# Conditioning projection of a two-block transformer kernel: as two-column products among the attention units, or as a GpSimd sum beside the feed-forward

## The chip, the cores and the metric
One NeuronCore of one Trainium2 chip runs the whole program in one launch. The metric is device microseconds of an execution, median of the runs. The engines are TensorE (PE, with weight loads shown as PEld), VectorE (DVE), ScalarE (ACT), GpSimd (POOL) and SyncE (SP), which issues most DMAs. Each runs its own instructions in program order and waits on semaphores for the others.

## What is computed
Two layers of a first block, then one layer of a second block, on 512 tokens of 1024 features, in float32. The part that the change touches is `mod`, the conditioning projection that the second block needs at its beginning. It depends on the inputs alone, so it may be formed at any time before.

```python
def first_block(x, ...):
    for l in range(2):
        # three attentions on rms_norm(x): MLA (6 heads, 96 wide), differential
        # (4 heads x 2 maps, 64 wide, values 128 wide), GQA (6 query heads, 64 wide)
        x = x + mix @ w_o[l]
        gate, up = jnp.split(_rms_norm(x, ffn_norm[l]) @ w_gate_up[l], 2, axis=-1)
        x = x + (jax.nn.silu(gate) * up) @ w_down[l]        # 2816 hidden

def second_block(x, c, ctx, c_ctx, w_ada, b_ada, ...):
    mod   = (silu(c)     @ w_ada[0] + b_ada[0])[:, None, :]  # 6 * 1024 values
    mod_c =  silu(c_ctx) @ w_ada[0] + b_ada[0]               # the first 2 * 1024 are used
    sh1, sc1, g1, sh2, sc2, g2 = jnp.split(mod, 6, axis=-1)
    ...
```

## The kernel before
Activations lie feature-major: 8 tiles of 128 features by 512 tokens. Each engine's order is written out by hand, in one function for each engine, and counters of semaphores tie them together.

A layer of the first block runs: input projection (split into high and low float32r parts), then three attentions one after the other, differential, GQA, MLA, then the output projection, then the feed-forward (FFN). An attention is a loop over units (`attend` on PE, `softmaxes` on ACT): one unit is one head or map by 128 queries, 32 units in the differential attention, 24 in GQA and in MLA. In step j PE transposes the exponentials of unit j (4 transposes of 128x128), forms the scores of unit j + 3 (one product of 512 columns in float32, of 64 rows in the differential attention and in GQA, of 96 in MLA), and multiplies values for unit j - 1 (4 products, 128 columns wide in the differential attention, 64 in GQA and MLA). DVE finds each row's maximum, ACT takes the exponential and copies the transposes out of PSUM. An attention is entered through a block of transposes that bring heads into feature-major form, which ACT copies out.

The 48 x 128 columns of `w_ada` go through the three-slot weight `ring` in 24 pieces of 256 columns (`ada_piece`, 1 MB each), 12 a layer, between the MLA weights and `w_o`. `modulation` on PE takes one: 8 products with `cvec`, the two silu'd vectors, as the stationary operand of two columns, 256 columns moving. ACT copies the 2x256 row out, `modulation_columns` transposes it in two 2-row transposes, and ACT copies 128x4 into `mod`. One piece is taken ahead of an attention's first scores, and three more at the steps of `ADA_AT`.

The FFN has 38 pieces of weights, 22 of gate and up (q < FT) and 16 halves of down. SP loads raw weights into two buffers `raws`, ACT copies the high part (`split_high`), DVE subtracts (`split_low`), PE multiplies, three float32r products for each tile (48 a gate/up piece, 33 a down half). SP issues the load of piece q when the split of piece q - 2 is done. POOL has no work in the FFN; it forms the low parts of the input weights, rotates GQA's and MLA's heads, and issues the small loads.

Of the kernel before, what the change touches and what calls it, by code (L numbers as in the profile page):

```python
# [80 lines left out]
def build(nc, A, out):  # L81
    ctx = ExitStack()
    with ctx:
# [6 lines left out]

        xT = sb("xT", [P, KT, S])
        C = sb("C", [P, 2944])
        ident = sb("ident", [P, P])
# [81 lines left out]
        ptmp = R[:, 11904:12288].rearrange("p (a c) -> p a c", a=2)  # L175
        mod_row = R[0:2, 12544:12800]
        SQ = R[:, 13056:14208].rearrange("p (a c) -> p a c", a=2)
# [95 lines left out]

        ADA_AT = {(32, 0): (3, 12, 22), (24, 32): (2, 9, 16), (24, 56): (2, 9, 16)}
        AW = 256

# [20 lines left out]
        piece_high, piece_low = sem("piece_high"), sem("piece_low")  # L297
        c_in = sem("c_in")
        gqa_inv_ready = sem("gqa_inv_ready")
        bT_ready, gT_ready, aT_ready = sem("bT_ready"), sem("gT_ready"), sem("aT_ready")  # L300
# [45 lines left out]
        def quarter_pieces(what, a, n):  # L346
# [6 lines left out]
                + quarter_pieces("gqa_kv", c1 + 3 * BH * BV + GH * GD, 2 * GK * GD))  # L353
        L_PIECES = len(W_IN) + 2 + 6 * D // AW // L + len(WO[0])

# [5 lines left out]
        def layer_pieces(l):  # L361
            w = A["w_in"][l]
            for _, a, n in W_IN:
                yield lambda i, a=a, n=n: [(slot(i, KT, n), cols(w, a, a + n))]
            yield lambda i: [(slot(i, 3, AH * AQK), cols(A["mla_w_uq"][l], 0, AH * AQK))]
            yield lambda i: [(slot(i, 2, AH * 128), cols(A["mla_w_ukv"][l], 0, AH * 128))]
            for a in range(NADA):
                yield ada_piece(l * NADA + a)
# [3 lines left out]
        def ada_piece(a):  # L372
            return lambda i: [(slot(i, KT, AW), cols(A["w_ada_2"][0], a * AW, (a + 1) * AW))]

        NADA = 6 * D // AW // L

# [97 lines left out]
        def _(pool):  # L474
# [67 lines left out]
            for l in range(L):  # L542
# [13 lines left out]
                for t in range(TT):  # L556
                    norm_rope_A(pg, nc.gpsimd, l, t, ptmp)

            pg.more(x_ready, KT * 2 * L)
            pool.dma_start(tribias, A["c_tribias"]).then_inc(tab_in, 16)  # L560
# [15 lines left out]
        def _(pe):  # L576
# [67 lines left out]

            def modulation():

                i = weights()
                bank = ab.fill(pe)
                group(ab, bank[0:2, 0:AW], [(cvec[:, k, :], slot(i, KT, AW)[:, k, :]) for k in range(KT)]).then_inc(a_full, 1)
                read_by.append((a_full, ab.n))  # L650
                return ab.n

            def modulation_columns(taken):

                pe.wait_ge(a_free, taken)
                bank = ab.fill(pe)
                for m in range(AW // P):
                    ins = nc.tensor.transpose(bank[:, 2 * m:2 * m + 2], mod_row[:, m * P:(m + 1) * P], ident[0:2, 0:2])
                ins.then_inc(a_full, 1)

            def attend(units, l):
# [16 lines left out]

                evacuated = ab.n
                rows_taken = modulation()  # L680
                pe.wait_ge(a_free, evacuated)
                if u0 >= 1:
# [23 lines left out]
            def layer(l):  # L706
# [58 lines left out]
                read_by.append((a_full, ab.n))  # L765
                if l == 0:
                    pp.more(cs_ready)
                attend([(QK[c * 64:c * 64 + 64, h, t * P:(t + 1) * P], QK[c * 64:c * 64 + 64, 4 + h, :],
# [44 lines left out]
            def ffn(l, sums):  # L813
# [16 lines left out]
                for q in range(NF):  # L830
# [9 lines left out]
                    else:  # L840
# [7 lines left out]
                        if a == 0:  # L848
                            ins.then_inc(half_read, 1)
                            f_by.append((half_read, l * KT + (q - FT) // 2 + 1))  # L850
                        else:
                            ins.then_inc(d_full, 1)
                            f_by.append((d_full, db.n))
                            if (q - FT) // 2 >= 2:
                                sums = norm_sums(X, TT, [(q - FT) // 2 - 2], sums)
                norm_sums(X, TT, [KT - 2, KT - 1], sums)

            for l in range(L):
# [271 lines left out]
        def _(sp):  # L1130
# [13 lines left out]
            def load_ffn(l):  # L1144
                up_down = FFN_W[l]
                sp.wait_ge(*read_by[(n - 1) // NSLOT * NSLOT])
                for q in range(NF):
# [25 lines left out]
        def _(act):  # L1173
# [10 lines left out]
            raw_count = [0, 0]  # L1184
            ada = 0

# [19 lines left out]
            def softmaxes(N):  # L1206
                nonlocal unit, ada
                u0 = unit
# [5 lines left out]

                def take_rows():
                    bank = ab.take(act)
                    copy_out(mod_row, bank[0:2, 0:AW], a_free)

                take_rows()
                columns_due = True  # L1220
                expo(u0)
                expo(u0 + 1)
                for j in range(N):
# [3 lines left out]
                    copy_out(PTb[:, (u0 + j) % 2, :], bank[:, :], a_free)  # L1227
                    if columns_due:
                        bank = ab.take(act)
                        copy_out(mod[:, 2 * ada:2 * ada + 2, :], bank[:, 0:4].rearrange("p (a b) -> p a b", b=2), a_free)  # L1230
                        ada += 1
                        columns_due = False
                    if j in ADA_AT[N, unit % 80]:
                        take_rows()
                        columns_due = True
                unit += N
# [105 lines left out]
            def ffn_silu(l):  # L1342
# [18 lines left out]
                for q in range(NF):  # L1361
# [8 lines left out]
                    if q >= FT and (q - FT) % 2:  # L1370
                        square((q - FT) // 2)

            for l in range(L):
# [152 lines left out]
        def _(dve):  # L1526
# [4 lines left out]
            vp.do(v.memset(eps[:, :], EPS), setup)  # L1531
            vp.do(v.memset(ss[:, :, :], 1.0))

            def set_gains():
# [204 lines left out]
            sh1, sc1, g1, sh2, sc2, g2 = range(0, 48, KT)  # L1739
            dve.wait_ge(vec_in, 16 * N_VEC)  # L1740
            vp.do(v.tensor_tensor(mod[:, :, :], mod[:, :, :], bc(bada[:, :], 2, 2), ALU.add))
            for j, (g, sc, c) in enumerate(((0, sc1, 0), (0, sc1, 1), (1, sc2, 0))):
# [252 lines left out]
```

## Time and profile before

| | us |
|---|---|
| median of 3 runs | 3435.35 (3433.83 to 3438.79) |
| profiled execution, span from first to last instruction | 3426.4 |
| median less the span | 8.95 |
| PE busy in the span | 3252.0 (95%) |
| DVE, ACT, POOL busy | 1119.9, 995.3, 279.3 |
| share of the chain that ended last on PE | 89% |

The time of an execution is measured around the program, so it is a little above the span of a profiled one. The trace gives each instruction's start and length, and for idle time of an engine what released it. The chain of waits is followed back from the last instruction, so a stretch of it on PE is time that nothing hides. The granted clock of PE has two levels, 1.00 for 2.4 GHz and 0.50 for 1.2 GHz. The mean over the span is 0.959. A float32 product shows in the trace as two instructions of each kind, so 8 products are x16.

### The profile page before, as it was taken

What the parts mean: (1) busy time and instruction counts of PE and PEld (TensorE: products, weight loads), DVE (VectorE), ACT (ScalarE), POOL (GpSimd) and SP (SyncE); (2) the same over time, 40 slices, a digit from 0 to 9 for tenths busy, and PEclk for the clock granted to TensorE, in tenths of its full rate; (3) what the DMA queues carried; (4) which work ended last, traced back from release to release, by engine and by line L of the source; (5) the groups of instructions that cost most, each with busy time, mean ns of one, the idle gap of its engine ahead of it and who ended that gap; (6) DMA issues with size and microseconds to landing.
All of it is one profiled execution on the core that took longest, in us unless ns stands there. A gap on an engine that the chain in (4) does not pass through costs nothing.

```text
span 3426.4 us, 35084 instructions
## 1 busy us (share of the span) xinstructions
PE 3252.0 (95%) x14020; PEld 2219.0 (65%) x14020; DVE 1119.9 (33%) x1827; ACT 995.3 (29%) x1607; POOL 279.3 (8%) x268
## 2 busy tenths in 40 slices
PE   7999998999989999989999999979998999989997
PEld 6866564888878656658887555544666433468886
DVE  2624332333226343233332233344333100043322
ACT  4355441222233545322221223333222100022222
POOL 4480000000032700000000000000000000000000
PEclk8999999999989999999999999989998999989999
DMA  4221121333222211123323201102111121123331
GB/s 105 79 80 38 38 75 37 99 98 88 85 82 76 74 38 53 47 78 96 93 84 92 80 14 36 37 1 62 37 37 50 25 74 49 49 62 98 95 90 62
DMA packets 340274, 221.98 MB, mean 65 GB/s; under 512 B 8364, under 2 KB 334892, under 8 KB 340112
## 3 DMA queue, kind: packets, MB, share of 16 engines
q1 hardware_dynamic: 337360, 214.65, 21.6%
q0 software_dynamic: 2224, 2.99, 0.8%
q8 instruction: 112, 1.84, 0.2%
q10 hardware_dynamic: 528, 2.10, 0.2%
q14 instruction: 50, 0.41, 0.0%
HBM read 217.62 MB, written 2.10 MB: 64 GB/s over the span
## 4 chain that ended last, share of the span: by engine, by line
PE 89%; DVE 5%; ACT 4%; issue 1%; DMA 1%; DVEq 0%; ACTq 0%; SPq 0%
PE ps L591 83%; PE ps L602 4%; PE ps L618 2%; DVE R L1691 1%; ACT R L1204 1%; DVE xL L1687 0%; DVE x_lows L1687 0%; DMA ident<-in_c_ident 0%; PE ps L945 0%; DMA R<-in_ctx 0%; ACT R L1200 0%; ACT L1193 0%; DVE R L1780 0%; DVE R L1762 0%; DVE wL L1713 0%
## 5 line engine op out<-in xcount | busy, mean ns | idle before, releaser
L591 PE MATMUL ps<-R 128*128 128x64 f32 (+6 forms) x2272 | 519.6, 372 | 29.5 <-ACT R L1204 8.7
L591 PEld LDWEIGHTS ps<-R 128*128 128x128 f32 (+3 forms) x2272 | 306.1, 192 | 243.8 <-issue 137.1
L591 PE MATMUL ps<-xH,wH 128*128 128x512 f32 x1056 | 417.5, 395 | 21.9 <-DVE xL L1687 21.9
L591 PE MATMUL ps<-U,ring 128*128 128x512 f32 (+5 forms) x960 | 406.8, 575 | 12.3 <-ACT R L1410 12.3
L1204 ACT ACTIVATE R<-ps 128x512 f32<-128x512 f32 (+9 forms) x504 | 248.7, 493 | 578.7 <-PE ps L591 514.6
L591 PE MATMUL ps<-xL,wH 128*128 128x512 f32 x1056 | 414.2, 392 | 0.0
L591 PE MATMUL ps<-xH,wL 128*128 128x512 f32 x1056 | 414.0, 392 | 0.0
L591 PE MATMUL ps<-R,ring 128*128 128x512 f32 x704 | 367.2, 676 | 2.9 <-DVE R L1927 1.6
L1354 ACT ACTIVATE wH<-raws 128x2048 fp32r<-128x2048 f32 (+1 forms) x114 | 192.9, 1692 | 569.0 <-PE ps L591 568.4
L591 PEld LDWEIGHTS ps<-U,ring 128*128 128x128 f32 (+2 forms) x960 | 179.6, 191 | 214.7 <-issue 189.5
L1713 DVE TENSOR_TENSOR wL<-raws,wH 128x2048 fp32r<-128x2048 f32 (+1 forms) x114 | 229.3, 2011 | 233.2 <-ACT wH L1354 226.3
L591 PEld LDWEIGHTS ps<-R,ring 128*128 128x128 f32 x704 | 133.4, 193 | 203.3 <-issue 199.1
L591 PEld LDWEIGHTS ps<-xH,wH 128*128 128x128 f32 x1056 | 199.9, 189 | 77.8 <-issue 20.2
L591 PE MATMUL ps<-ring_parts,U_parts 128*128 128x256 f32 (+1 forms) x1152 | 215.2, 290 | 15.1 <-DVE x_lows L1687 15.1
L591 PEld LDWEIGHTS ps<-xH,wL 128*128 128x128 f32 x1056 | 200.2, 190 | 41.8
L591 PEld LDWEIGHTS ps<-xL,wH 128*128 128x128 f32 x1056 | 200.4, 190 | 40.4
L591 PE MATMUL ps<-hH,wH 128*128 128x512 f32 x528 | 207.2, 392 | 0.0
L591 PE MATMUL ps<-ring,U 128*128 128x256 f32 x768 | 189.8, 392 | 17.8 <-DVEq L55 17.3
L591 PE MATMUL ps<-hH,wL 128*128 128x512 f32 x528 | 205.7, 390 | 0.0
L591 PE MATMUL ps<-hL,wH 128*128 128x512 f32 x528 | 205.5, 389 | 0.0
L591 PEld LDWEIGHTS ps<-ring_parts,U_parts 128*128 128x128 f32 x1152 | 184.2, 197 | 22.0 <-issue 12.3
L591 PEld LDWEIGHTS ps<-ring,U 128*128 128x128 f32 x768 | 142.9, 193 | 59.8 <-issue 20.3
(279 smaller groups left out, 3281.8 us busy)
## 6 DMA issues: line engine op xcount, KB each, us to landing
raws<-in_w_gate_up SPq DMA_DIRECT2D x88, 512.0 KB, 5.1
ring<-in_w_in SPq DMA_DIRECT2D x36, 1024.0 KB, 6.2
ring<-in_w_ada SPq DMA_DIRECT2D x24, 1024.0 KB, 5.1
raws<-in_w_down SPq DMA_DIRECT2D x32, 704.0 KB, 4.6
raws<-in_w_ffn_in SPq DMA_DIRECT2D x44, 512.0 KB, 5.2
ring<-in_w_in SPq DMA_DIRECT2D x34, 512.0 KB, 5.7
raws<-in_w_ffn_out SPq DMA_DIRECT2D x16, 704.0 KB, 4.7
ring<-in_w_o SPq DMA_DIRECT2D x5, 1280.0 KB, 5.9
```

The source lines that it names most:

```text
L591: return nc.tensor.matmul(o, a, b, start=first, stop=last)
L602: ins = nc.tensor.transpose(bank[0:rows_, t * P:(t + 1) * P], v, ident[:, :])
L618: ins = nc.tensor.matmul(bank[:, t:t + 1], src(k)[:, t * P:(t + 1) * P], ones[:, 0:1], start=k == 0 and t == 0, stop=k == KT - 1, skip_gro ...
L1204: ap.do(f(dst, src, ACT.Copy), sem)
L1354: ap.do(f(wH[:, g % 2, 0:n], raws[:, g % 2, 0:n], ACT.Copy), wh_ready)
L1691: vp.do(v.scalar_tensor_tensor(t, xT[:, k, :], gain(k), inv, ALU.mult, ALU.mult), scaled if shift is None else None)
L1713: vp.do(v.tensor_tensor(wL[:, g % 2, 0:n], raws[:, g % 2, 0:n], wH[:, g % 2, 0:n].bitcast(F32), ALU.subtract), wl_ready)
```

## The change
The 24 products with `cvec` and their transposes leave the attentions, and the ada pieces leave the ring. In the two FFNs of the first block, behind the products of weight pieces q = 5 to 28, there is now one ada piece each: a column tile of 128 outputs for one of the two vectors, 24 a layer (`ADA`: tiles 0 to 15 for both vectors, 16 to 47 for the first alone). SP loads it (512 KB) into one of two buffers `ada_raw`, behind the raw weights of q, after the piece two before has been read. POOL multiplies its 8 x 128 columns by the 8 values of the vector and adds halves three times (512, 256, 128 columns). PE multiplies the 128x128 result by a column of ones into bank 7, and ACT copies one column into `mod`. Layers end with PE waiting for the last of these reads, and DVE waits for all 48 ahead of its use of `mod`. POOL's scratch for DMA descriptors is halved to make room for the buffers.

```diff
-        ADA_AT = {(32, 0): (3, 12, 22), (24, 32): (2, 9, 16), (24, 56): (2, 9, 16)}
-        AW = 256
+        ADA = [(m, 0) for m in range(16)] + [(m, 1) for m in range(16)] + [(m, 0) for m in range(16, 48)]
+        ADA_FIRST, N_ADA = 5, len(ADA) // L
...
+        def ada_at(l, q):
+            a = l * N_ADA + q - ADA_FIRST
+            return a if l < L and 0 <= q - ADA_FIRST < N_ADA else None
...
+                pool.wait_ge(cs_ready, 1)
+                for a in range(l * N_ADA, (l + 1) * N_ADA):
+                    w = ada_half(a)
+                    pool.wait_ge(ada_in[a % 2], 16 * (a // 2 + 1))
+                    w_ = w.rearrange("p (k c) -> p k c", k=KT)
+                    pg.do(nc.gpsimd.tensor_tensor(w_, w_, bc(cvec[:, :, ADA[a][1]], P, 2), ALU.mult))
+                    for n in (4, 2, 1):
+                        pg.do(nc.gpsimd.tensor_tensor(w[:, 0:n * P], w[:, 0:n * P], w[:, n * P:2 * n * P], ALU.add),
+                              ada_summed if n == 1 else None)
...
-                group(ab, bank[0:2, 0:AW], [(cvec[:, k, :], slot(i, KT, AW)[:, k, :]) for k in range(KT)]).then_inc(a_full, 1)
...
+            def modulation(a):
+
+                pe.wait_ge(ada_summed, a + 1)
+                if a >= 1:
+                    pe.wait_ge(ada_read, a)
+                mm(psum[7][:, 0:1], ada_half(a)[:, 0:P], ones[:, 0:1], True, True).then_inc(ada_full, 1)
...
-                evacuated = ab.n
-                rows_taken = modulation()
-                pe.wait_ge(a_free, evacuated)
+                pe.wait_ge(a_free, ab.n)
...
-                    if rows_taken:
-                        modulation_columns(rows_taken)
-                        rows_taken = None
-                    if j in ADA_AT[N, unit % 80]:
-                        rows_taken = modulation()
...
+                    if ada_at(l, q) is not None:
+                        a = ada_at(l, q)
+                        if a >= 2:
+                            sp.wait_ge(ada_read, a - 1)
+                        sp.dma_start(ada_half(a).rearrange("p (k c) -> p k c", k=KT),
+                                     cols(A["w_ada_2"][0], ADA[a][0] * P, (ADA[a][0] + 1) * P)).then_inc(ada_in[a % 2], 16)
...
+                    if ada_at(l, q) is not None:
+                        m, c = ADA[ada_at(l, q)]
+                        ap.more(ada_full)
+                        ap.do(f(mod[:, m, c:c + 1], psum[7][:, 0:1], ACT.Copy), ada_read)
```

PE at the start of GQA in the first layer, before. `ps0` to `ps2` take transposes and ada products, `ps5` to `ps7` scores, `ps3` and `ps4` values; a row with `ident` is transposes.

```order
L602 MATMUL ps2<-ident,R 64x128 x4
L591 MATMUL ps0<-ring,cvec 2x256 x8
L591 MATMUL ps7<-R 128x512
L591 MATMUL ps5<-R 128x512
L591 MATMUL ps6<-R 128x512
L602 MATMUL ps1<-ident,R 128x128 x4
L591 MATMUL ps7<-R 128x512
L658 MATMUL ps2<-ident,R 128x2 x2
L602 MATMUL ps0<-ident,R 128x128 x4
L591 MATMUL ps5<-R 128x512
L591 MATMUL ps4<-R 128x64 x4
```

The same place in the changed kernel.

```order
L616 MATMUL ps0<-ident,R 64x128 x4
L605 MATMUL ps7<-R 128x512
L605 MATMUL ps5<-R 128x512
L605 MATMUL ps6<-R 128x512
L616 MATMUL ps1<-ident,R 128x128 x4
L605 MATMUL ps7<-R 128x512
L616 MATMUL ps2<-ident,R 128x128 x4
L605 MATMUL ps5<-R 128x512
L605 MATMUL ps4<-R 128x64 x4
```

The product with `cvec` between the transposes and the first scores, and the two column transposes behind the fourth, are gone; all else keeps its order. PE in the first layer's FFN, behind gate/up piece 5, in the changed kernel:

```order
L605 MATMUL ps4<-xH,wH 128x512
L605 MATMUL ps4<-xL1,wH 128x512
L605 MATMUL ps4<-xH,wL 128x512
L605 MATMUL ps7<-ones,ada_raw 128x1
L605 MATMUL ps0<-xH,wH 128x512
L605 MATMUL ps0<-xL0,wH 128x512
L605 MATMUL ps0<-xH,wL 128x512
```

One product of one column now stands between two pieces; before, the row with `ps0` followed the one with `ps4`. SP from the MLA weights on in the first layer, before:

```order
L1141 DMA ring<-in_mla_w_ukv 128x2x768
L1141 DMA ring<-in_w_ada_2 128x8x256 x12
L1141 DMA ring<-in_w_o 128x10x384 x2
L1141 DMA ring<-in_w_o 128x10x256
L1154 DMA raws<-in_w_gate_up 128x8x128 x44
```

And in the changed kernel, from the last `w_o` piece on:

```order
L1141 DMA ring<-in_w_o 128x10x256
L1154 DMA raws<-in_w_gate_up 128x8x128 x12
L1164 DMA ada_raw<-in_w_ada_2 128x8x128
L1154 DMA raws<-in_w_gate_up 128x8x128 x2
L1164 DMA ada_raw<-in_w_ada_2 128x8x128
L1154 DMA raws<-in_w_gate_up 128x8x128 x2
```

The ada loads moved from the ring, ahead of `w_o`, to behind the raw weights of each of 24 FFN pieces, and so ahead of the raw weights of the next one.

## Rows read from the trace of the kernel before

**Rows 1.** Chain in order of time, first layer's differential attention: start us, us, what
```profile
243.99 5.68 PE ps L591 x26
...
253.20 2.14 PE ps L591 x10
...
255.78 2.14 PE ps L591 x10
```

**Rows 2.** Timeline, MLA start: start us, us, engine, line, operation, tiles
```profile
424.00 4.35 ACT L1204 ACTIVATE R<-ps 96x512 f32<-96x512 f32 x7
...
430.79 2.84 PE L591 MATMUL ps<-R 96*128 96x512 f32 x6
```

**Rows 3.** Timeline, GQA start in the first layer; in brackets idle before, and releaser
```profile
337.42 0.31 ACT L1331 ACTIVATE ssO<-ssO,eps 128x16 f32<-128x16 f32 x1
...
339.15 1.28 ACT L1212 ACT_TABLE_LOAD   x1 [1.02 <-DVE nmax L1589]
...
341.28 1.11 PE L602 MATMUL ps<-ident,R 128*128 128x128 f32 x4 [1.22 <-ACT R L1212]
```

**Rows 4.** Windows: stretch, us, PE, PEld, DVE, ACT, POOL busy, PE's clock, DMA
```profile
231.40:242.00 10.60, 10.57 (x28) 5.74 (x28) 2.46 (x5) 4.33 (x11) 9.74 (x12) 0.50 0.01 2
341.20:354.30 13.10, 13.02 (x36) 7.41 (x36) 1.83 (x4) 5.11 (x13) 0.00 (x0) 0.50 0.04 13
354.30:358.10 3.80, 3.80 (x10) 1.10 (x10) 1.14 (x3) 0.00 (x0) 0.00 (x0) 0.50 0.00 0
358.20:359.70 1.50, 1.50 (x8) 0.42 (x5) 0.00 (x0) 0.00 (x0) 0.00 (x0) 1.00 0.00 0
1259.30:1272.40 13.10, 13.03 (x36) 7.41 (x36) 1.83 (x4) 5.10 (x13) 0.00 (x0) 0.50 0.05 15
1272.40:1276.20 3.80, 3.80 (x10) 1.10 (x10) 1.14 (x3) 0.00 (x0) 0.00 (x0) 0.50 0.00 0
```

**Rows 5.** Chain in order of time, first layer's GQA, to MLA's transposes
```profile
329.30 4.30 PE ps L602 x32
...
345.74 3.90 PE ps L591 x10
...
350.50 9.29 PE ps L591 x26
...
385.03 2.09 PE ps L591 x10
...
387.56 2.09 PE ps L591 x10
...
420.34 6.82 PE ps L602 x48
```

**Rows 6.** Timeline, PE at the second layer's differential start
```profile
1146.73 3.62 PE L591 MATMUL ps<-ring,cvec 128*2 128x256 f32 x16
...
1154.41 0.66 PE L602 MATMUL ps<-ident,R 128*128 128x128 f32 x4 [1.30 <-ACT R L1212]
```

**Rows 7.** Chain in order of time, down projection of the first layer
```profile
893.36 15.13 PE ps L591 x66
909.27 15.13 PE ps L591 x66
```

**Rows 8.** Groups by form, POOL: line, operation, tiles, count, busy us, mean ns
```profile
L440 POOL TENSOR_TENSOR R<-R 128x384 f32<-128x384 f32 x8 | 8.0, 996 | 0.6
...
L440 POOL TENSOR_TENSOR R<-R 128x128 f32<-128x128 f32 x8 | 3.6, 453 | 0.6
```

**Rows 9.** Timeline, input projection of the second layer, DVE beside POOL
```profile
963.72 4.50 POOL L537 TENSOR_TENSOR ring_parts<-ring,ring_parts 128x2048 fp32r<-128x2048 f32 x1 [699.18 <-ACT ring_parts L1251]
...
965.47 3.31 DVE L1687 TENSOR_TENSOR x_lows<-R,U_parts 128x512 fp32r<-128x512 f32 x1
...
969.59 0.69 DVE L1687 TENSOR_TENSOR x_lows<-R,U_parts 128x512 fp32r<-128x512 f32 x1
```

**Rows 10.** Page, DMA issues: tiles, queue, count, KB each, us to landing
```profile
raws<-in_w_gate_up SPq DMA_DIRECT2D x88, 512.0 KB, 5.1
```

More of the change, by code:

```diff
@@ L91, in build @@
         xT = sb("xT", [P, KT, S])
+        ada_raw = sb("ada_raw", [P, 2, KT * P])
         C = sb("C", [P, 2944])
@@ L175, in build @@
         ptmp = R[:, 11904:12288].rearrange("p (a c) -> p a c", a=2)
-        mod_row = R[0:2, 12544:12800]
         SQ = R[:, 13056:14208].rearrange("p (a c) -> p a c", a=2)
@@ L298, in build @@
         c_in = sem("c_in")
+        ada_in = [sem("ada_in0"), sem("ada_in1")]
+        ada_summed, ada_full, ada_read = sem("ada_summed"), sem("ada_full"), sem("ada_read")
         gqa_inv_ready = sem("gqa_inv_ready")
@@ L353, in build @@
                 + quarter_pieces("gqa_kv", c1 + 3 * BH * BV + GH * GD, 2 * GK * GD))
-        L_PIECES = len(W_IN) + 2 + 6 * D // AW // L + len(WO[0])
+        L_PIECES = len(W_IN) + 2 + len(WO[0])
         def piece_parts(i, n):
@@ L366, in layer_pieces, with ada_half @@
             yield lambda i: [(slot(i, 2, AH * 128), cols(A["mla_w_ukv"][l], 0, AH * 128))]
-            for a in range(NADA):
-                yield ada_piece(l * NADA + a)
             for a, e in WO[l]:
                 yield lambda i, a=a, e=e: [(slot(i, 10, e - a), cols(A["w_o"][l], a, e))]
-        def ada_piece(a):
-            return lambda i: [(slot(i, KT, AW), cols(A["w_ada_2"][0], a * AW, (a + 1) * AW))]
-        NADA = 6 * D // AW // L
+        def ada_at(l, q):
+            a = l * N_ADA + q - ADA_FIRST
+            return a if l < L and 0 <= q - ADA_FIRST < N_ADA else None
+        def ada_half(a):
+            return ada_raw[:, a % 2, :]
         def second_pieces():
@@ L643, in tokens @@
                         .then_inc(ring_.filled, 1)
-            def modulation():
-                i = weights()
-                bank = ab.fill(pe)
-                group(ab, bank[0:2, 0:AW], [(cvec[:, k, :], slot(i, KT, AW)[:, k, :]) for k in range(KT)]).then_inc(a_full, 1)
[L650 to L659, printed above, removed]
+            def modulation(a):
[3 more added lines that the diff above has]
+                mm(psum[7][:, 0:1], ada_half(a)[:, 0:P], ones[:, 0:1], True, True).then_inc(ada_full, 1)
             def attend(units, l):
@@ L765, in layer @@
                 read_by.append((a_full, ab.n))
-                if l == 0:
-                    pp.more(cs_ready)
                 attend([(QK[c * 64:c * 64 + 64, h, t * P:(t + 1) * P], QK[c * 64:c * 64 + 64, 4 + h, :],
@@ L855, in ffn @@
                                 sums = norm_sums(X, TT, [(q - FT) // 2 - 2], sums)
+                    if ada_at(l, q) is not None:
+                        modulation(ada_at(l, q))
                 norm_sums(X, TT, [KT - 2, KT - 1], sums)
+                if l < L:
+                    pe.wait_ge(ada_read, (l + 1) * N_ADA)
             for l in range(L):
@@ L1184, in _ @@
             raw_count = [0, 0]
-            ada = 0
             def square(k):
@@ L1206, in softmaxes @@
             def softmaxes(N):
-                nonlocal unit, ada
+                nonlocal unit
                 u0 = unit
@@ L1213, in expo @@
                             accum_out=rsum[:, u % 4:u % 4 + 1]), s_exp)
[L1215 to L1220, printed above, removed]
                 expo(u0)
@@ L1227, in softmaxes @@
                     copy_out(PTb[:, (u0 + j) % 2, :], bank[:, :], a_free)
[L1228 to L1235, printed above, removed]
                 unit += N
@@ L1371, in ffn_silu @@
                         square((q - FT) // 2)
+                    if ada_at(l, q) is not None:
+                        m, c = ADA[ada_at(l, q)]
+                        ap.more(ada_full)
+                        ap.do(f(mod[:, m, c:c + 1], psum[7][:, 0:1], ACT.Copy), ada_read)
             for l in range(L):
@@ L1532, in _ @@
             vp.do(v.memset(ss[:, :, :], 1.0))
+            vp.do(v.memset(mod[:, 16:48, 1:2], 0.0))
             def set_gains():
@@ L1740, in _ @@
             dve.wait_ge(vec_in, 16 * N_VEC)
+            dve.wait_ge(ada_read, len(ADA))
             vp.do(v.tensor_tensor(mod[:, :, :], mod[:, :, :], bc(bada[:, :], 2, 2), ALU.add))
@@ L1983 @@
     from concourse.bass_utils import run_bass_kernel_spmd
-    nc = bacc.Bacc("TRN2", target_bir_lowering=False, num_devices=1)
+    nc = bacc.Bacc("TRN2", target_bir_lowering=False, num_devices=1, dynamic_dma_scratch_size=8192)
     arrays, views = {}, {}
```

## The prediction
> **What bounds the kernel now.** TensorE (PE) is busy 95% of the span, and the chain of waits that ended last lies on it for 89%, so I asked of each stage that the diff touches what PE itself pays there. First the chain in order of time through the attentions. In the first layer's differential attention [rows 1] a unit without an ada product takes 255.78 - 253.20 = 2.58 us, and PE never waits in it. The unit with a product and the one after it, which carries its column transposes, take 253.20 - 243.99 = 9.21 us. One ada piece thus costs 9.21 - 2 x 2.58 = 4.05 us of PE's own time, and nothing hides it. The other two attentions repeat the pattern at 2.53 us (GQA, [rows 5]) and 2.14 us (MLA) a unit, with the same 4.05 for a piece. Then the starts of the attentions [rows 2, 3, 6], where PE waits for ScalarE (ACT), and the table of windows with PE's granted clock [rows 4].
>
> That table decides the case. At the start of the first differential attention PE stands still up to 231.40 and its clock has fallen to 0.50 (the 1.2 GHz level); it works 10.57 of 10.60 us at that level and is back at 2.4 GHz at 242. At the start of GQA the clock falls too. There PE works 13.02 of 13.10 us at 0.50, with no ada product in it, and the clock doesn't come back. It comes back at about 358.1, while the ada product runs (354.30 to 358.10 at 0.50, 358.20 to 359.70 at 1.00). The second layer does the same: 13.03 of 13.10 us of attention units at 0.50, then the product, and in it the return at about 1276.3. So in both layers what PE did when the clock rose in GQA was the ada product, and no GQA unit was ever seen to bring it back. GQA units at full clock do keep it [rows 5].
>
> **What is removed.** 24 pieces: 4 in each of six attentions, one ahead of the first scores and three among the units.
> - Differential, both layers: 3 x 4.05 = 12.15, and for the first piece only its column transposes, 0.3, since the first exponential waits for ACT and VectorE (DVE), not for the product: -12.45 each, **-24.9**.
> - MLA, both layers: 12.15 again. Its first product stands ahead of the scores, which start at 430.79 [rows 2]; without it they wait only for ACT's last copy, 424.00 + 4.35 = 428.35, so they start 2.3 earlier; with the transposes 2.7. -14.85 each, **-29.7**.
>
> **GQA, the term that turns the sign.** Its start first [rows 3]: ACT ends the root at 337.42 + 0.31 = 337.73, and then waits for a maximum of scores that stood behind the product; table load to first transposes takes 341.28 - 339.15 = 2.13. Without the product the scores are there by then, and PE begins at about 337.77 + 2.13 = 339.90, 1.38 earlier. But PE has then stood still longer: its transposes end at 329.30 + 4.30 = 333.60 [rows 5], three score products follow, and then nothing until 339.9, where before it had only the 1.22 us ahead of 341.28. The clock fell even with the product there, so I take it to fall again, in both layers. Now nothing like the product follows. A GQA unit at 0.50 takes 350.50 - 345.74 = 4.76 us [rows 5] against 387.56 - 385.03 = 2.53. All 24 at the low level: 24 x 4.76 = 114.2, less the score products that the last three units don't have (three take some 2.6 at full clock, [rows 2], 5.1 at half) = 109.1. End 339.90 + 109.1 = 449.0, where before it was 420.34: +28.7. The method holds for before: 24 x 2.53 - 2.6 = 58.1, pieces 3 x 4.05 + 0.3 = 12.5, and half of the 16.8 us at 0.50 (341.28 to 358.1) = 8.4, together 79.0; the trace has 420.34 - 341.28 = 79.1. Two layers: **+57.4**. MLA's transposes, 48 in a row, then begin at the low level; they are dense and of full height, and I take the clock to return in them; some 5 us of them at half clock that ACT's copies would otherwise allow faster: 1.8 each, **+3.6**.
>
> The Trainium skill, "TensorE: Matmul & The Clock Gate", section "Part 1: The HAM clock gate", says that the default state is throttled and that sustained matmul activity releases it. Read as "PE without gaps", it has GQA back at full clock about as soon as the differential attention. By that rule this term would be -33.8 in place of +57.4; the 13 us of gapless work at 0.50 in each layer [rows 4] speak against that reading.
>
> **Differential attention of the second layer.** Before, PE had a product up to 1146.73 + 3.62 = 1150.35 and only 1.30 us of idle ahead of its first transposes [rows 6], and the clock stayed at 1.00. Without the product it stands still from 1146.73 to 1154.41 but for three score products. The nearest row is the first layer's start, with its stop before 231.40. Bounds: 0 if the clock holds, 5.3 if it costs what 10.6 us at half clock do [rows 4]. I take **+5.0**. The first layer's start has this loss already.
>
> **What is added, in the two feed-forwards (FFN) of the first block.** PE: 48 products with a one-column moving operand. The nearest is the sum of squares, four of them between two down-projection tiles: 909.27 - 893.36 - 15.13 = 0.78 us [rows 7], 0.195 each; the upper bound is that each one alone costs all 0.78. 9.4 or 37; I take the lower since the four have the same shape and also interrupt a stream: **+9.5**.
> GpSimd (POOL) [rows 8]: its adds take 453 ns at 128 elements and 996 at 384, so 2.1 ns an element more: 0.45, 0.73 and 1.27 us for the adds of 128, 256 and 512, and 2.36 for the multiply of 1024, if its broadcast costs nothing more. 4.8 us a piece, 5.1 with its waits. Pieces come once in a gate/up tile (48 products x 0.229 = 11 us) or a down half (15.13 / 2 + 0.4 + 0.2 = 8.2), on an engine that has nothing else there.
> SP: each ada load stands ahead of the next raw weight load and waits for the read of the piece two before, which ACT does after its split of the next weights, some 2.4 us into a tile. Load 5 to 6 us [rows 10], with the raw load beside it. A piece then is ready at about 2.4 + 0.4 + 5.7 + 5.1 = 13.6 us, wanted after two down halves, 16.4; the raw weights behind it land 9 us in and are split 4 us later, wanted at 16.4 too. Slack 2.8 us, in gate/up 8. ACT's 48 copies of one column lie in its idle time.
> DVE: one row shows a subtraction with both inputs in SBUF taking 3.31 us where it takes 0.69 [rows 9]; it ended 0.56 us after the POOL operation beside it. So a POOL multiply can hold up DVE's low split, and DVE's 1.6 to 2.3 us split can hold up a POOL step: up to 2 us each, within the slack. The Trainium skill, "SBUF — State Buffer", section "SBUF: two separate sides", has the same as a lock held for a whole instruction, not a shared rate; the trace agrees with the lock. Shared at equal rates, the subtraction would have lost 0.7, not 2.6, and neither changes the sum.
> The smaller scratch for POOL's own DMAs can only delay POOL's small loads; the rotations that follow them are not wanted before GQA, some 60 us later: 0, and a few us if that cover failed.
>
> **The sum** against the profiled execution: -24.9 - 29.7 + 57.4 + 3.6 + 5.0 + 9.5 = +20.9 on its span of 3426.4. The median is 8.95 above that span, and this rest stays. 3435.35 + 20.9 = **3456 us**.
>
> **Rivals.**
> - GQA comes back to full clock without a product (the skill's reading, or since the clock doesn't fall). For it: full-clock GQA units hold the clock, and the differential units brought it back. Against: [rows 4], twice. Price a layer: 339.90 + 58.1 + 5.3 of a start at half clock = 403.3, so -17.0, and the 3.6 of the transposes gone: 20.9 - 57.4 - 34.0 - 3.6 = -74, **3361 us**. This is the other side. The point from which it decides: without GQA the sum is -40, so the sign turns where a layer's GQA costs +20, that is 37 us more than here, 16.6 units at 2.23 beyond the 2.4 units' worth of its start: with fewer than 19 of the 24 units at half clock the change gains. Chance 0.11.
> - The same in one layer only: 3456 - 47 = **3409 us**. 0.05.
> - The FFN loop is longer than two down halves (POOL and DVE hold each other up at each step, loads land late). 2 us over in each of 14 pairs: **3484 us** at most, about 3470 with half of it. 0.09.
> - MLA starts at, or falls to, the low level too and stays there, as GQA does: its units have 64-column products as well. About 2 us for each of 24 units, 48 a layer: **3552 us**. 0.04.
> The rest, 0.71, is the forecast. That the change doesn't do what it says is no case: the products are gone from the attentions' order and stand in the feed-forwards'.
>
> **Range.** The forecast's own terms give 3456 with -12 (5.0 and 3.6 at zero, the clock's return by chance a few us sooner) and +27 for the one-column products at their upper bound. 3440 to 3484 holds it and the FFN rival, 0.80; outside are both faster cases and the MLA one. A measurement tells 0.2%, some 7 us: faster 0.16, within 0.04, slower 0.80.
>
> **What would show it.** Granted clock 0.50 through all of GQA in both layers, units at 4.76, 1.00 again within MLA's transposes; differential and MLA units at 2.58 and 2.14 with no 9.21 pairs; a fall of the clock at the second layer's first start. In FFN 48 POOL groups of about 5 us and PE idle near none in front of ps<-ada_raw. I am wrong if the clock in GQA is at 1.00 after some 10 us, or if PE waits for POOL.

## The result, and the profile after

| | before | after |
|---|---|---|
| median, us (runs) | 3435.38 (4) | 3465.05 (4) |
| lowest to highest | 3433.83 to 3438.79 | 3459.97 to 3467.24 |
| profiled span | 3426.4 | 3465.4 |
| mean granted clock | 0.959 | 0.926 |

The changed kernel is slower: ratio 1.0084, 95% interval 1.0070 to 1.0099. The forecast was 3456 (3440 to 3484), slower. The profiled executions differ by 39.0 us, the medians by 29.7; more on that below.

First a correction. The text on record counts 48 ada pieces, 24 a layer, behind q = 5 to 28. The list `ADA` has 16 + 16 + 32 = **64** entries: tiles 0 to 15 for both vectors and 16 to 47 for one. So there are 32 pieces a layer, behind q = 5 to 36, 17 in gate/up and 15 in the down halves, and DVE waits for 64. The page of after has the count:

```profile
L568 POOL TENSOR_TENSOR ada_raw<-ada_raw,cvec 128x1024 f32<-128x1024 f32 x64 | 123.8, 1935 | 1047.4 <-DMA ada_raw<-in_w_ada 1047.4
```

Windows of after, PE alone (stretch, us, PE busy, PE's clock, DMA): GQA of the first layer, MLA's transposes behind it, the second layer's differential start, GQA of the second layer.

```profile
331.80:435.80 104.00, 104.00 (x325) 0.50 0.00 1
436.00:441.00 5.00, 5.00 (x25) 0.51 0.01 3
1161.30:1181.00 19.70, 19.70 (x45) 0.50 0.15 51
1264.80:1372.00 107.20, 107.19 (x330) 0.50 0.00 1
```

These answer to [rows 4]. Before, the stretch at 0.50 ended inside the ada product. Now PE works 104.00 of 104.00 us and 107.19 of 107.20 without a gap, and stays at the 1.2 GHz level to the end of GQA. The Trainium skill, "TensorE: Matmul & The Clock Gate", "Part 1: The HAM clock gate", has sustained matmul activity release the throttle. Read as "PE is busy", the trace refutes it twice; which products are at work when the clock does rise is asked below.

The chain of after at the start and the end of the first layer's GQA:

```profile
330.11 0.66 PE ps L616 x4
...
332.86 3.90 PE ps L605 x10
...
337.62 3.90 PE ps L605 x10
```

```profile
427.08 0.85 PE ps L616 x4
...
436.14 5.03 PE ps L616 x24
```

A unit takes 337.62 - 332.86 = 4.76 us, as in the slow pair of [rows 5], all the way. GQA's first transposes to MLA's take 436.14 - 330.11 = 106.0 us, against 420.34 - 341.28 = 79.1 before.

Stage by stage, the two profiled executions:

| stage | change, us | predicted |
|---|---|---|
| differential, first layer | -10.8 | -12.45 |
| GQA, first layer (with its start) | +25.5 | +28.7 |
| MLA, first layer (with its transposes) | -13.7 | -13.05 |
| all attentions and projections of the second layer | +7.5 | +8.2 |
| FFN, first layer | +10.8 | +4.7 |
| FFN, second layer | +10.6 | +4.7 |
| second block and last FFN, from the loading of `ctx` on | +8.1 | 0 |

An attention is counted from the block of transposes ahead of it to the next one's, MLA to the FFN's first product. The 1.0 us that the table lacks lies ahead of the first differential attention. Within the second layer the differential attention changed by -5.2, GQA by +26.9, MLA by -13.4, and what is ahead of them by -0.8.

### The profile page after: what moved, and what is told of

It reads as the page before. It is cut to its first block, busy times and chain, and to the rows that moved or that the text cites. A ratio compares the mean times of both kernels' runs of the same rounds, so it can differ in the third digit from the quotient of the medians.

```text
span 3465.4 us, 34885 instructions
## 1 busy us (share of the span) xinstructions
PE 3281.0 (95%) x13716; PEld 2267.4 (65%) x13716; DVE 1136.1 (33%) x1828; ACT 992.6 (29%) x1623; POOL 604.9 (17%) x524
## 4 chain that ended last, share of the span: by engine, by line
PE 83%; DVE 5%; ACT 5%; DMA 5%; issue 1%; POOL 0%; SPq 0%; ACTq 0%; DVEq 0%; POOLq 0%
PE ps L605 77%; DMA raws<-in_w_down 4%; PE ps L616 4%; PE ps L632 1%; ACT wH L1345 1%; ACT R L1209 1%; DVE R L1687 1%; DVE xL L1683 0%; DVE x_lows L1683 0%; DVE wL L1709 0%; DMA ident<-in_c_ident 0%; PE ps L945 0%; DMA R<-in_ctx 0%; DMA ada_raw<-in_w_ada 0%; ACT L1198 0%
## 5 line engine op out<-in xcount | busy, mean ns | idle before, releaser
L605 PE MATMUL ps<-R 128*128 128x64 f32 (+6 forms) x2272 | 601.4, 416 | 36.5 <-ACT R L1209 16.1
L605 PEld LDWEIGHTS ps<-R 128*128 128x128 f32 (+3 forms) x2272 | 353.6, 220 | 287.5 <-issue 161.6
L1209 ACT ACTIVATE R<-ps 128x512 f32<-128x512 f32 (+8 forms) x480 | 239.4, 499 | 520.0 <-PE ps L605 448.1
L1709 DVE TENSOR_TENSOR wL<-raws,wH 128x2048 fp32r<-128x2048 f32 (+1 forms) x114 | 239.0, 2096 | 298.7 <-ACT wH L1345 291.9
L568 POOL TENSOR_TENSOR ada_raw<-ada_raw,cvec 128x1024 f32<-128x1024 f32 x64 | 123.8, 1935 | 1047.4 <-DMA ada_raw<-in_w_ada 1047.4
L570 POOL TENSOR_TENSOR ada_raw<-ada_raw 128x512 f32<-128x512 f32 (+2 forms) x192 | 201.6, 1050 | 15.1
```

Source lines behind the costliest of these rows:

```text
L568: pg.do(nc.gpsimd.tensor_tensor(w_, w_, bc(cvec[:, :, ADA[a][1]], P, 2), ALU.mult))
L570: pg.do(nc.gpsimd.tensor_tensor(w[:, 0:n * P], w[:, 0:n * P], w[:, n * P:2 * n * P], ALU.add), ada_summed if n == 1 else None)
L605: return nc.tensor.matmul(o, a, b, start=first, stop=last)
L1209: ap.do(f(dst, src, ACT.Copy), sem)
L1709: vp.do(v.tensor_tensor(wL[:, g % 2, 0:n], raws[:, g % 2, 0:n], wH[:, g % 2, 0:n].bitcast(F32), ALU.subtract), wl_ready)
```

## Experiments

Each kernel below is the changed one with one edit, unless it says otherwise. Runs of before beside them: 3434.14 (10 runs), 3434.81 (9) and 3435.19 (9).

### A tall product in GQA, and a low one

Is it the ada product that brought the clock back, and what about it? In step 3 of each GQA:

```diff
+ bank = ab.fill(pe)
+ for n in range(8):
+     c = n % 4 * 256
+     mm(bank[0:2, 0:256], ones[0:rows, 0:2], V[0:rows, n // 4, c:c + 256], True, True)
```

with rows = 128 ("tall") and rows = 64 ("low").

> The changed kernel plus 8 products in each GQA attention, ahead of the transposes of its fourth unit: 2 stationary columns (of the ones), 256 moving columns, 128 rows high, float32, result not read. This is the shape of the ada product that was taken away. Theory 1 (GQA's units, with scores and transposes' outputs only 64 rows or columns, don't bring the clock back, the tall product did): the clock rises during the product, about 354 in the first layer, and the units behind it take 2.53 us. A layer's GQA then takes about 3 x 4.75 + 6 + 20.5 x 2.53 = 72 us in place of 106, and MLA's transposes start at full clock: 2 x 34 + 3.6 less, about 3394 us. Theory 2 (something else in the removed edit held the clock, for instance the column transposes, the extra copies on ACT, or the traffic of the ring): the clock stays at 0.50 and the time is 3465 + 2 x 6.8 = 3479.

> As the one with 8 added products in each GQA, with the same columns and the same time on PE, but 64 rows high in place of 128. Theory 1a (the clock's return goes by how many of the array's rows work): it stays at 0.50 through GQA in both layers, and the time is 3465 + 2 x 6.8 = 3479. Theory 1b (it goes by long stretches of moving columns between short pieces, whatever their height): the clock returns as with the tall product, about 3394 us.

Measured: tall **3392.22** us (0.988 of before, 0.9865 to 0.9895), low **3480.18** (1.0133, 1.0119 to 1.0147). The expectations were 3394 and 3479. The chain of tall, then of low:

```profile
336.93 9.34 PE ps L606 x26
346.27 0.59 PE ps L617 x4
346.87 2.09 PE ps L606 x10
...
349.40 2.09 PE ps L606 x10
```

```profile
338.20 10.81 PE ps L606 x26
...
350.06 3.90 PE ps L606 x10
...
354.82 3.90 PE ps L606 x10
```

The piece x26 is the product with its neighbours. Behind the tall one units take 2.53 us, behind the low one 4.76, with the same columns and PE equally without gaps. So the return needs neither the column transposes, nor ACT's copies, nor the ring's traffic, and PE's busy time doesn't decide it. Of two products alike in columns, in place and in leaving no gap, the one 128 rows high brought full clock in both layers, the one 64 rows high in neither. The low run shows where it came instead. The last three units of a GQA have no score product left, only transposes and value products, all 128 rows high and the latter still 64 columns wide. The last score product ends at 432.9, MLA's transposes begin at 441.15 (1381.85 in the second layer), and between them the clock rises:

```profile
433.00:438.00 5.00, 5.00 (x26) 0.50 0.00 0
438.10:441.10 3.00, 3.00 (x28) 1.00 0.00 0
...
1380.20:1381.80 1.60, 1.60 (x16) 1.00 0.00 0
```

Five profiled kernels leave GQA with its low scores and without a tall product (after, low, and three of the runs below: no_ada, pe_only, copy_first). In their ten GQAs the clock rose four times in these last units and six times in MLA's transposes, never in a unit with a score product of 64 rows. So values 64 columns wide don't keep the clock down by themselves. Nor does a score product of 64 rows: the differential units have one too, beside values 128 columns wide, and among them the clock came back at 246.4 in after. How the one weighs against the other within a unit isn't shown.

The removed product repaired the clock as a side effect, and one product of some 4 us was worth (3465.05 - 3392.22) / 2 = 36 us a layer, its own time paid.

### GQA's scores made tall with zeros

If height counts, the scores themselves can be made tall at no cost in instructions:

```diff
+ # DVE, unit 8 of the differential attention
+ vp.do(v.memset(QK[64:128, 13:16, :], 0.0), pad_ready)
...
+ pe.wait_ge(pad_ready, l + 1)
- attend([(QK[0:64, 8 + h, t * P:(t + 1) * P], QK[0:64, 14 + h // 3, :],
+ attend([(QK[:, 8 + h, t * P:(t + 1) * P], QK[:, 14 + h // 3, :],
```

> The changed kernel with GQA's score products made 128 rows high in place of 64, in both layers: the lower half of the array gets zeros as keys (one VectorE write of zeros a layer, beside the differential attention) and old finite data as queries, so the result is the same, the instructions on TensorE are as many and as long, and no product is added. Theory 1 (the clock's return goes by how many of the array's rows a product occupies, and zeros count): GQA starts at 0.50 and is back at full clock after some 15 to 20 us; a layer's GQA takes about 67 us in place of 106, 2 x 39 + 3.6 less: 3383 us. Theory 2 (rows fed with zeros don't count, or the long tall product was needed): no change, 3465 us.

The zeros stand in the keys; the queries have old finite values in these rows. Measured: **3354.58** us (0.9766, 0.9753 to 0.978), 110.5 less than the changed kernel, where 82 was expected; the two GQAs are 53.5 and 56.7 us shorter in the profiles. Windows, PE alone, then the chain:

```profile
334.00:338.00 4.00, 4.00 (x12) 0.60 0.00 0
338.20:384.00 45.80, 44.81 (x302) 1.00 0.01 1
1195.00:1240.00 45.00, 40.52 (x263) 1.00 0.00 1
```

```profile
336.61 2.55 PE ps L606 x10
339.16 0.44 PE ps L617 x4
339.60 1.70 PE ps L606 x10
341.30 0.45 PE ps L617 x4
341.75 1.70 PE ps L606 x10
```

Rows of zeros serve as well. The clock dips for some 3 us at the first layer's start and not at all in the second. And a unit takes 341.75 - 339.60 = 2.15 us, not 2.53: a score product 64 rows high costs 0.38 us more than one of 128, which I had not expected. That is 24 x 0.38 x 2 = 18 of the 28 us beyond the expectation; most of the rest is the earlier return. Weight loads at one unit, in tall (scores 64 high) and here:

```profile
349.33 0.29 PEld L606 LDWEIGHTS ps<-R 64*128 64x128 f32 x2 [0.17 <-issue]
350.38 0.97 PEld L606 LDWEIGHTS ps<-R 128*128 128x128 f32 x8 [0.76 <-issue]
```

```profile
350.05 0.30 PEld L606 LDWEIGHTS ps<-R 128*128 128x128 f32 x2
350.66 0.19 PEld L606 LDWEIGHTS ps<-R 128*128 128x128 f32 x1 [0.31 <-DVE U L1651]
```

With 64 rows the next product's weights are loaded 1.05 us after the scores' load began, with 128 rows 0.61 after. The Trainium skill, "TensorE: Matmul & The Clock Gate", "Part 2: What happens when you issue a matmul", lets a weight load be pulled ahead of products in flight where row groups don't conflict, or where it goes to the background weight buffer. That doesn't tell the two cases apart: the next load is 128 rows high in both and meets rows of the score product in both. Why the load comes later behind 64 rows stays open; the runs show that it does, and what it costs.

### The change without the clock's part

Before, with the same tall scores in GQA and nothing else changed:

> The kernel before with only GQA's scores made 128 rows high (zeros), in both layers. Theory: it gains 24 x 0.39 a layer from the shorter units (2.14 us in place of 2.53) and some 6.5 a layer from an earlier return of the clock at GQA's start, 3434.5 - 18.7 - 13 = 3402.8. Then the change, with the same scores at 3354.6, gains 48 us: its sign hung on the clock alone. Rival (a score product of 128 rows is worth more than that here, or the ada products among the units take up what it gains): 3380 or 3430, and the change would gain 25 or 75.

Measured: **3413.14** us (0.9939, 0.9926 to 0.9951), 10 above the 3403 expected. GQA itself behaved. The chain of the first layer:

```profile
347.61 0.66 PE ps L603 x4
...
410.86 6.82 PE ps L603 x48
```

From its first transposes to MLA's it takes 63.3 us, 15.8 less than before, and the second layer's GQA gives the same. Some of it went again in the differential attentions, which took 3.3 and 5.5 us more than in before's profile, the clock falling at other places: in the second layer 1147.80 to 1157.80 is at 0.50, where before's profile had full clock [rows 6].

```profile
1147.80:1157.80 10.00, 10.00 (x30) 0.50 0.00 0
```

With tall scores in both, the change gives 3413.14 to 3354.58, **-58.6 us**, where 48 was expected. That is what its own terms give without the clock: -24.9 and -29.7, the same pieces in GQA -24.9, and +20.8 of FFN (see the section on the feed-forward), together -58.7. That it agrees to 0.1 is luck, since medians of one kernel move by more; the two profiles have it stage by stage, the first and the second layer: differential -12.6 and -12.5, GQA -12.2 and -14.0, MLA -15.6 and -14.7, FFN +10.9 and +9.7 (62.3 in all, with before's tall version profiled in its slowest run).

### Filling the standstill instead

Small products whose result isn't read, ahead of the first scores or the first transposes of an attention:

```diff
+ for n in range(k):
+     mm(bank[0:2, 0:P], ones[:, 0:2], ident[:, :], True, True)
```

> The changed kernel with small products whose result is not read (2 stationary columns, 128 moving, 128 rows high, float32, about 0.21 us each) where TensorE would stand still: 44 in the second layer and 40 + 18 in the first ahead of the differential attention's first transposes, and 5 ahead of GQA's first scores and 9 behind them, in both layers. Theory 1 (it is the standstill at the start that lets the clock fall): no fall at these starts, GQA runs at 2.53 us a unit from the first, 2 x 48 + 3.6 less, the differential attentions 5 and 8 less: 3352 us. Rival (the fill of some 3 us in GQA's start is too little, the clock falls there and then nothing brings it back): only the differential attentions gain, about 3452 us.

Measured: **3373.04** us (0.982, 0.9806 to 0.9833): between the two, much nearer to theory 1. The clock holds through the first layer's attentions and both layers' GQA. Windows over the first layer's GQA start and GQA, and of the second layer's differential start, where it fell all the same:

```profile
319.00:334.00 15.00, 14.80 (x83) 1.00 0.00 1
334.00:390.00 56.00, 54.99 (x328) 1.00 0.00 1
...
1122.40:1135.80 13.40, 13.40 (x36) 0.50 0.00 0
```

So with the standstill at GQA's start filled, its long stretch at the low clock never begins: the GQAs are 47.1 and 48.5 us shorter than in after, as forecast (48). The fillings are 128 rows high, so whether the missing gap or the tall products held the clock isn't told apart. The size was missed in the differential attentions. The first layer's gained 1.7 us where 8 was forecast, and the second layer's lost 5.3 where 5 was to be gained, for I had given its start too much filling. The timeline there:

```profile
1107.91 9.77 PE L606 MATMUL ps<-ident,ones 128*2 128x128 f32 x88
...
1111.84 0.33 ACT L1333 ACTIVATE rsA<-ss,eps 128x48 f32<-128x48 f32 x1 [0.71 <-DVEq L55]
...
1117.61 2.84 PE L606 MATMUL ps<-R 64*128 64x512 f32 x6
```

ACT had made its last copy before 1111.84, but the scores stood behind the filling until 1117.61: some 6 us lost on the path by my reading, with another wait and a fall of the clock behind them. I had read the chain's long stretch on ACT as idle time of PE, and much of it was PE's own products, paced by ACT.

### The feed-forward: pieces left out, and TensorE's part alone

> The changed kernel without the ada pieces at all (no loads, no GpSimd sums, no one-column products, no copies): the product with w_ada is left out, and mod is formed from b_ada alone. Theory: the two feed-forwards of the first block fall back to the 381.4 us of before, 2 x 10.7 less, and the 8 us of the second block, where the same instructions run and only the clock fell in other places, stay or move by a few us at random: 3444 us. Rival: the second block's 8 us hang on the ada pieces too (their time shifts or their late loads): 3436 us.

> The changed kernel with only TensorE's and ScalarE's part of the ada pieces: the 64 one-column products with the identity as stationary operand, and the 64 copies; no ada loads and no GpSimd sums, so that the product with w_ada is left out and mod is a constant and b_ada. Theory (the predicted 0.195 us for each product): 12.5 us dearer than without any ada piece, about 3456, the other 9 us of the feed-forwards being waits of PE for GpSimd and for late loads. Rival (each interruption of the stream costs PE 0.33 us, and the waits are hidden): 3465, as with all.

Measured: without ada pieces (no_ada) **3444.27** (1.0031, 1.0019 to 1.0042), as forecast; with one-column products and copies alone (pe_only) **3459.84** (1.0074, 1.0061 to 1.0086), between the theory's 3456 and the rival's 3465. So all of FFN's loss is 3465.05 - 3444.27 = 20.8 us; 15.6 of it are the 64 one-column products, **0.243** each, and 5.2 what loads and GpSimd add. The profiles say the same more sharply. From its first product to its last, an FFN takes 369.09 us in before, 369.07 and 369.10 without the pieces, 376.68 in both layers with TensorE's part alone, and 379.86 and 379.64 in after. That is 7.6 a layer or 0.237 for each product, and 3.2 and 3.0 beside. The attentions' part is 3444.27 - 3434.14 = +10.1, where +11.4 was predicted. The second block's 8 us stay without the pieces, from the load of `ctx` on (3442.7 - 1882.1 = 1560.6 in its profile, 3426.4 - 1874.05 = 1552.35 in before's), so they aren't the pieces' doing. Nor are they the change's: before with tall scores has 1559.8 there, and the other profiled kernels 1557.7 to 1563.8. Before's profile is the odd one.

### The copy's place on ScalarE

The chain of after in the down halves leaves PE:

```profile
882.44 5.88 DMA raws<-in_w_down
...
888.43 1.39 ACT wH L1345
...
891.12 5.93 DMA raws<-in_w_down
...
897.16 1.39 ACT wH L1345
...
898.58 0.18 ACT mod L1366
...
898.77 0.37 SPq L1164
...
899.18 5.87 DMA raws<-in_w_down
```

A raw load, ACT's split, ACT's copy of the ada column, SP's next ada load, and the next raw load: 8.1 to 8.7 us, about the length of a down half (8.2). The chain puts the raw load at 891.12 down to DVE's split, but there too ACT's copy ended at 890.69 and SP issued the ada load at 890.71. The page of after has the raw loads of the down projection, and those of the same size in the last FFN, which has no ada loads:

```profile
raws<-in_w_down SPq DMA_DIRECT2D x32, 704.0 KB, 5.9
...
raws<-in_w_ffn_out SPq DMA_DIRECT2D x16, 704.0 KB, 4.6
```

```diff
+ if ada_at(l, q) is not None: ...ap.do(f(mod[:, m, c:c + 1], psum[7][:, 0:1], ACT.Copy), ada_read)
  if q + 2 < NF:
      split_high(q + 2)
...
- if ada_at(l, q) is not None: ...
```

ACT's copy stood behind the split of weights two pieces on; now it stands ahead of it.

> The changed kernel with ScalarE's copy of an ada column moved ahead of its split of the next raw weights, instead of behind it. As it stands the copy of piece q waits for the landing of raw weights q + 2, the next ada load waits for the copy, and the next raw load stands behind that ada load on SyncE, so each down half costs one raw load and one split, 8.3 to 8.7 us. Theory (this loop is what is left of the feed-forwards' loss beside the one-column products): the loop is gone, the feed-forwards lose 2 x 2.6 us less, 3460 us as with the one-column products alone. Rival (GpSimd's four steps, which VectorE holds up, are late by themselves, or the loads merely are slower side by side): 3465 us.

Measured: **3457.91** us (1.0068, 1.0055 to 1.0082), 7.1 less than with the copy behind, and no more than with TensorE's part alone. The runs of the two overlap (after 3459.97 to 3467.24, this one 3455.49 to 3461.96), but the profiles settle it: the FFNs take 376.68 us in both layers, to 0.01 what they take with TensorE's part alone. The loop cost 3.2 + 3.0 = 6.1 us, and the copy's place was all of it. The chain of the same stretch is PE again:

```profile
879.82 5.89 PE ps L605 x26
885.72 0.79 PE ps L632 x8
886.50 15.56 PE ps L605 x70
902.06 0.79 PE ps L632 x8
```

PE's waits for `ada_raw` are gone too; in after's first FFN the waits of PE had them at the top:

```profile
PE ps L605 <- POOL ada_raw L570: 2.2, 4, 0.9
```

So the four GpSimd steps were not late by themselves; they were started late.

### Together

> The three edits together: GQA's scores 128 rows high with zeros, the small products where TensorE would stand still, and the copy of the ada column ahead of the split. If all three theories hold, 3352 - 5 = 3347 us; if the fill fails to hold the clock at GQA's start but the tall scores bring it back, 3383 - 13 - 5 = 3365 us; if neither works, 3447 us.

> The changed kernel with GQA's scores 128 rows high (zeros) and the copy of the ada column ahead of the split, without the small products in the idle time. The earlier run with all three took 3352.6, no less than the tall scores alone, 3354.6. Theory: the small products, which ended behind the gap that they were to fill, cost what the copy's place gained, so without them 3354.6 - 7.1 = 3347.5. Rival: with GQA at full clock the copy's place is worth nothing, 3354.6.

> As pad_copy2, and the differential attention's score products 128 rows high too: the queries of the two maps lie in tiles of their own whose other 64 rows are zeros (written by GpSimd), against the keys of both maps. 4 more copies a layer on ScalarE at the attention's start (about 2.4 us). Theory (a product of 64 rows keeps the weight loads next to it from overlapping, 0.39 us a unit, and brings the clock back late): 32 x 0.39 less a layer, 2.4 more, and some 8 us less of the first layer's start at half clock: 3347 - 25 + 5 - 8 = 3319. Rival (the 0.39 is a matter of GQA's 64 columns of values, not of the scores' rows; the differential units, with 128 columns, are bound by their 12 products and keep 2.58): 3347 + 5 = 3352.

Measured: the three edits together **3352.6** (0.9759, 0.9746 to 0.9773); without the fillings **3351.27** (0.9755, 0.9741 to 0.9768); the intervals overlap. The profiles tell more: beside tall scores the fillings make the first layer's differential attention and GQA 1.7 and 1.6 us shorter and the second layer's differential attention 7.8 longer. The copy's place shows as -3.3 in the medians, within what these runs can tell (those without the fillings go from 3347.01 to 3351.87), but the FFNs go from 380.02 and 378.82 us to 376.67 and 376.70, so its 5.5 is there with tall scores as well. With the differential scores tall too: **3325.53** (0.9682, 0.9669 to 0.9695), 25.7 less again, where 28 was expected. It beats both kernels, before by 3.2%. Chain of its first layer's differential attention:

```profile
239.32 1.71 PE ps L609 x2
...
241.88 2.44 PE ps L609 x10
...
244.75 1.75 PE ps L609 x10
...
246.94 1.75 PE ps L609 x10
```

2.19 us a unit in place of 2.58 [rows 1]: the 0.39 goes with the scores' height, not with the width of the values, and full clock is there in the third unit.

## Where the prediction was right and where not

- **The sign and its reason.** Right. GQA stayed at 0.50 in both layers; the product that was removed had been what brought the clock back. Tall and low runs show it, at 3392 and 3480.
- **GQA, +28.7.** Measured +25.5 and +26.9. The units are as forecast, 4.76. The start came as forecast too (10.55 us behind the differential attention's last product, for 11.98 - 1.38 = 10.60), though not by the path drawn: the three score products don't follow the transposes at once, they wait 1.24 us for ACT's copies. The length, 106.0, was put 3.1 too long. The clock fell only at 331.7, when the first transposes and a score product were done, 1.6 us in, while I had counted all 24 units at the low level. And a unit without its score product takes 429.53 - 427.08 = 2.45 us, 2.31 less than the others, where I had taken off 1.7, three times.
- **Differential and MLA, -24.9 and -29.7.** The pieces' price was right, and with tall scores on both sides the stages show it. In this change the first layer's differential attention gained 10.8 for 12.45, since the clock came back 13.9 us after PE's start there, where in before it was 10.6. MLA with its transposes gained 13.7 and 13.4, for 14.85 - 1.8 = 13.05.
- **The second layer's differential start, +5.0.** The clock does fall there, and for longer than I took: 19.7 us at 0.50 in the window above, where the nearest row had 10.6. The attention changed by -5.2, so against its pieces' -12.45 the start cost 7.2. The layer as a whole came out at +7.5 for +8.2.
- **One-column products, +9.5.** The term that failed. The count was 48 for 64, and the price 0.195 for 0.243: [rows 7] has four in a row, and one alone between two streams costs more of its own. 64 x 0.243 = 15.6 by the medians, 15.2 by the profiles.
- **FFN's slack, 2.8 us.** The step that failed beside it. It had ACT's copy "after its split of the next weights, some 2.4 us into a tile", but didn't follow that the split itself waits for a raw load that stands behind the previous ada load on SP. That closes a loop of one raw load a half, and `raws` in the down projection land in 5.9 us where the same size takes 4.6 without the ada loads beside it. It cost 6.1 us in both layers together: the rival of the long FFN loop in small. The sign named against the forecast, PE waiting for POOL, was there too: 2.2 us in 4 waits in the first FFN, 1.1 in 2 in the second, all in the down halves.
- **The rest of 8.95.** Wrong reading. In every run that shows both, the time is 1.8 us above the span (3467.24 and 3465.4; before's timed runs, for instance 3434.89 and 3433.1). The other 7 us mean that before's profiled execution was a short one: 3426.4 + 1.8 = 3428.2, below all of before's timed runs (3430.73 at the least). Its second block took 1552.35 us, in after's profile 1560.45, and 1560.6 with the pieces left out. So the forecast of the median came out right by adding a difference, but the profiles' 39.0 must not be read as the change's effect.
- Against the medians, +29.7 where +20.9 was forecast, the attentions (10.1 for 11.4) came out 1.3 lower and the FFNs (20.8 for 9.5) 11.3 higher, together 10.0 for the 8.8 missed, which agrees within what the runs can tell. The sign didn't come by luck: it hung on GQA, and GQA did what was forecast. That the attentions' sum came within 1.3 is partly luck, GQA's 5 us too many against 4 us too few in the two differential attentions.
- A slip in the text on record: by its own prices the reading "PE without gaps" makes GQA's term -34.0, as the first rival has it, not -33.8.

## What to carry to other kernels

Before removing a product, ask what the clock does while it runs: one that costs 4 us of PE's time may be what lifts dozens of others from 1.2 to 2.4 GHz. A loop that never idles can stay at 1.2 GHz for its whole length; here it was one whose score products are 64 rows high. Try such operands at 128 rows, with zeros, where space allows. In GQA alone that gave before 0.6% and made the change itself a gain of 58.6 us in place of a loss of 29.7; with the change, the copy's new place and both attentions tall it came to 3.2% below before. And when work is laid beside a stream, follow every wait of each queue once around: a copy one statement too late closed a loop that cost 6 of the 21 us that the FFNs lost.

## What the runs showed that was not expected

- 104.00 us of 104.00 at the low clock with PE never idle. It ended in the transposes that followed, 128 rows high, or in other runs in the last three units, which have no score product; and rows of zeros serve as height.
- A float32 score product of 512 columns costs 0.38 to 0.39 us more in its unit at 64 rows than at 128 (2.53 against 2.15 in GQA, 2.58 against 2.19 in the differential attention). MLA's, 96 high, has units of 2.14.
- A GpSimd multiply of 128x1024 with a broadcast factor takes 1.94 us on average, less than the 2.36 worked out from its adds.
- Two executions of one kernel differ by up to 8 us (3430.7 to 3438.8 in before) with a mean granted clock of 0.958 in the shortest and 0.956 in runs at the long end (3437.78, 3438.57).
